# A weight block's residue made by POOL in two halves, each with its own semaphore, for a two-block network layer in split fp32

## What is computed

```python
def first_block(x, mem, ...):
    xn = rmsnorm(h, norm_mix_g); proj = xn @ w_in          # pool_mixer and sgu_mixer follow
    h = h + concatenate([y_pool, y_sgu]) @ w_out
    h = h + mem_cross_attention(rmsnorm(h, norm_xattn_g), mem, ...)   # wq, wk, wv, wo
    h = h + conv_ffn(rmsnorm(h, norm_ffn_g), w_up, conv_w, conv_b, w_down)
    return rmsnorm(h, final_norm_g)

def second_block(x, ...):
    h = rms_norm(x, norm1_g); proj = h @ w_in               # q, k, v, glu_a, glu_b
    x = x + concatenate([stick_breaking_attention(q, k, v), conv]) @ w_out
    gate, val = split(rms_norm(x, norm2_g) @ w_up)
    return x + (silu(depthwise_conv(gate)) * val) @ w_down
```

## Time and profile before

| | us |
|---|---|
| median of 3 runs | 1308.39 (1307.55 to 1308.89) |
| profiled execution, device time | 1306.23 |
| its span in the trace | 1304.5 |
| TensorE matmul busy (PE) | 1258.5 |
| VectorE busy (DVE) | 635.6 |
| POOL busy | 530.0 |
| ScalarE busy (ACT) | 485.4 |

### The profile page before, as it was taken

One profiled execution on the slowest core, in us unless ns is written; L12 is line 12 of the kernel. 1 busy time (PEld: TensorE's weight loads), 2 busy tenths in 40 slices (PEclk: granted clock), 3 DMA queues, 4 the chain that ended last, 5 costly groups with the idle time before them and its releaser, 6 DMA issues.

```text
span 1304.5 us, 16116 instructions
## 1 busy us (share of the span) xinstructions
PE 1258.5 (96%) x5574; PEld 1018.4 (78%) x5574; DVE 635.6 (49%) x882; ACT 485.4 (37%) x630; POOL 530.0 (41%) x244
## 2 busy tenths in 40 slices
PE   6899999999999999999979999799999999999999
PEld 6786888778888888888867776457888888888887
DVE  6829363353654155415585857694733313331332
ACT  6432342233443144314452234555533323332331
POOL 5854254223445344534454433000544353435343
PEclk9999999999999999999998999899999999999999
DMA  8432232112323222222232221000322232223222
GB/s 298 162 121 73 65 114 81 52 51 92 97 96 103 91 96 96 98 96 88 73 97 85 93 97 53 29 1 1 114 97 96 81 113 97 96 81 113 93 73 77
DMA packets 33313, 118.40 MB, mean 91 GB/s; under 512 B 3824, under 2 KB 3952, under 8 KB 32880
## 3 DMA queue, kind: packets, MB, share of 16 engines
q1 hardware_dynamic: 33120, 117.49, 27.1%
q10 hardware_dynamic: 144, 0.24, 0.1%
HBM read 115.61 MB, written 2.10 MB: 90 GB/s over the span
## 4 chain that ended last, share of the span: by engine, by line
PE 90%; DVE 6%; ACT 2%; issue 1%; DMA 0%; SPq 0%; DVEq 0%; ACTq 0%
PE ps L1028 25%; PE ps L1030 25%; PE ps L1029 25%; PE ps L1280 2%; DVE squares L625 2%; PE ps L1065 2%; PE ps L1066 2%; PE ps L1067 2%; PE ps L1263 1%; PE ps L1138 1%; PE ps L1160 1%; DVE slab L774 1%; DVE xg_lo L629 1%; PE ps L1307 1%; PE ps L1323 1%
## 5 line engine op out<-in xcount | busy, mean ns | idle before, releaser
L311 POOL TENSOR_TENSOR w_lo<-w_raw,w_hi 128x1024 fp32r<-128x1024 f32 x215 | 519.7, 2421 | 746.2 <-ACT w_hi L389 388.9
L1028 PE MATMUL ps<-xg_hi,w_hi 128*128 128x512 f32 x960 | 380.8, 397 | 10.4 <-DVE xg_lo L629 5.2
L1030 PE MATMUL ps<-xg_hi,w_lo 128*128 128x512 f32 x960 | 375.9, 392 | 0.0
L1029 PE MATMUL ps<-xg_lo,w_hi 128*128 128x512 f32 x960 | 375.7, 391 | 0.0
L1028 PE MATMUL ps<-y_hi,w_hi 128*128 128x512 f32 (+1 forms) x608 | 234.3, 385 | 13.6 <-DVE y_lo L629 10.8
L1030 PE MATMUL ps<-y_hi,w_lo 128*128 128x512 f32 (+1 forms) x608 | 231.5, 381 | 0.0
L1029 PE MATMUL ps<-y_lo,w_hi 128*128 128x512 f32 (+1 forms) x608 | 231.5, 381 | 0.0
L1028 PEld LDWEIGHTS ps<-xg_hi,w_hi 128*128 128x128 f32 x960 | 181.7, 189 | 51.4 <-DVE xg_lo L629 6.0
L1029 PEld LDWEIGHTS ps<-xg_lo,w_hi 128*128 128x128 f32 x960 | 181.8, 189 | 39.1 <-issue 1.7
L1030 PEld LDWEIGHTS ps<-xg_hi,w_lo 128*128 128x128 f32 x960 | 181.5, 189 | 38.3
L389 ACT ACTIVATE w_hi<-w_raw 128x1024 fp32r<-128x1024 f32 x136 | 143.1, 1052 | 160.3 <-PE ps L1030 126.5
(11 more groups left out here) (173 smaller groups left out, 1049.3 us busy)
## 6 DMA issues: line engine op xcount, KB each, us to landing
w_raw<-weights SPq DMA_DIRECT2D x200, 512.0 KB, 3.3
w_raw<-weights SPq DMA_DIRECT2D x16, 384.0 KB, 2.9
h<-x_t SPq DMA_DIRECT2D x2, 1024.0 KB, 11.7
out_t<-h SPq DMA_DIRECT2D x8, 256.0 KB, 2.0
slab<-mem_t SPq DMA_DIRECT2D x2, 512.0 KB, 6.1
slab<-mats_in SPq DMA_DIRECT2D x1, 1024.0 KB, 14.5
cols<-cols_in ACTq DMA_DIRECT2D x1, 231.0 KB, 4.3
corr<-corr_in SPq DMA_DIRECT2D x1, 32.0 KB, 14.4
```

What stands on the lines that cost most here:

```text
L311: nc.gpsimd.tensor_tensor(w_lo[:, s, :], w_raw[:, s, :], w_hi[:, s, :].bitcast(F32), ALU.subtract).then_inc(w_lo_ready, 1)
L1028: pe.matmul(out, w[0], x[0], start=first, stop=False)
L1029: pe.matmul(out, w[0], x[1], start=False, stop=False)
L1030: return pe.matmul(out, w[1], x[0], start=False, stop=last)
```

## The change

POOL subtracts in two instructions of 512 columns each; the first raises a new semaphore `w_lo_half`, the second the old `w_lo_ready`. VectorE's residue of block 0 is split in the same way. In `features` TensorE waits for `w_lo_half` at a block's start, and for `w_lo_ready` ahead of the first piece k of 4 or more; in `tokens` the first piece waits for `w_lo_half` and the second for `w_lo_ready`. SyncE's wait stays on `w_lo_ready`.

```diff
-        w_hi_ready, w_lo_ready = sem("w_hi_ready"), sem("w_lo_ready")
+        w_hi_ready, w_lo_half, w_lo_ready = sem("w_hi_ready"), sem("w_lo_half"), sem("w_lo_ready")
...
                 pool.wait_ge(w_hi_ready, b + 1)
-                nc.gpsimd.tensor_tensor(w_lo[:, s, :], w_raw[:, s, :], w_hi[:, s, :].bitcast(F32),
-                                        ALU.subtract).then_inc(w_lo_ready, 1)
+                for half, done in ((slice(0, BLK // 2), w_lo_half), (slice(BLK // 2, BLK), w_lo_ready)):
+                    nc.gpsimd.tensor_tensor(w_lo[:, s, half], w_raw[:, s, half], w_hi[:, s, half].bitcast(F32),
+                                            ALU.subtract).then_inc(done, 1)
...
-            nc.vector.tensor_tensor(w_lo[:, 0, :], w_raw[:, 0, :], w_hi[:, 0, :].bitcast(F32), ALU.subtract).then_inc(w_lo_ready, 1)
+            for part, done in ((slice(0, BLK // 2), w_lo_half), (slice(BLK // 2, BLK), w_lo_ready)):
+                nc.vector.tensor_tensor(w_lo[:, 0, part], w_raw[:, 0, part], w_hi[:, 0, part].bitcast(F32),
+                                        ALU.subtract).then_inc(done, 1)
...
                 if begin:
-                    pe.wait_ge(w_lo_ready, b + 1)
+                    pe.wait_ge(w_lo_half, b + 1)
...
                 for n, k in enumerate(order):
+                    if k >= DT // 2 and (n == 0 or order[n - 1] < DT // 2):
+                        pe.wait_ge(w_lo_ready, b + 1)
...
                 for s in range(4):
-                    pe.wait_ge(w_lo_ready, first + s + 1)
                     for kk in range(2):
+                        pe.wait_ge((w_lo_half, w_lo_ready)[kk], first + s + 1)
```

## The result

The changed kernel took 1300.08 us (1299.40 to 1300.61, 4 runs) beside 1307.97 us before (1306.75 to 1308.89, 4 runs): a ratio of 0.9942 [0.9927, 0.9957]. In two later comparisons the ratio was 0.9956 [0.9941, 0.9971] and 0.9958 [0.9944, 0.9971]. So it is faster, by 5.6 to 7.9 us, where I had forecast 2.6 us; 1300.08 lies under the low end of my range, 1302.6. The profiled execution took 1300.61 us (span 1298.9), 5.6 less than that of before.

The account below looks back on a forecast made before the run. TensorE, busy for 96% of the span, was taken as the bound, with VectorE setting the end in the hole. Terms -3.7 + 0.3 + 0.4 + 0.2, given as -2.6 us, put on the 1308.39 median: 1305.8 us, range 1302.6 to 1309.5.

Parts of the forecast that it names:

- the hole: Last down projection of the first feed-forward, 645 to 692 us: VectorE stands for half as long, -3.7 us.
- The stated effect: TensorE begins blocks with half the residue; its two `w_lo` waits of 2.6 us shrink, counted as no gain.
- the wait in mid-block: One more TensorE semaphore wait per block, 216 in all, taken as 0; third rival: stops the pipeline, 58 us, chance 0.03.
- 0.18 us a split: Extra POOL time for two instructions instead of one, making a half 1.29 us, between 1.20 and 1.40.
- the start: 25 to 45 us, where VectorE multiplies stand behind residues: plus 0.3 us, from -0.8 to 1.6.
- the pooling windows: 99 to 125 us, four residues among VectorE adds of two SBUF tiles: plus 0.4 us, from -0.3 to 1.1.
- The copy (L622): At the start, a VectorE copy newly stands behind part of the last half: 0.5 us taken, at most 1.29.
- the attention: Start of the attention, where L972 stands behind POOL and TensorE waits for its follower: plus 0.2 us, from 0 to 0.4.
- POOL keeps the port across both halves: First rival: VectorE cannot enter between halves, nothing gained, 18 pairs each 0.18 us longer, 1311.6 us; chance 0.12.
- the split costs 0.40: Second rival: the split costs near the power's 0.40 us, a half of 1.40, total 1309.2 us; chance 0.15.
- A clock gain in the hole: Fourth rival: shorter waits at 645 to 692 us keep TensorE at 2.4 GHz, up to 1.8 us more, 1304.0; chance 0.12.
- my first rival: POOL keeps SBUF's port through both halves, as consecutive POOL instructions are no barrier; 1311.6 us, chance 0.12.

Follow-up runs that it names:

- with the casts moved: Every residue in quarters as in the all-quarters kernel, with VectorE's two casts and mask multiply issued behind the first norm's reciprocal roots; 1301.86 us, ratio 0.9957 to before.

## Why the prediction was wrong

**What held.** The place, the mechanism and the order of size did. VectorE enters at the end of a half in the hole. The stated effect is worth nothing, as I had it (the split that waits for whole blocks gives 4.28 of 4.39 us), and so is the wait in mid-block (1.0005, unchanged). A half alone lasts 1.29 us in the median, the value I took; two take 2.54 where a whole one took 2.40, so 0.14 us for the instruction more. The estimate from the page GPSIMD Engine Reference of the Trainium skill, section 3.1 (Elementwise, side-by-side cycle accounting), was 0.30 and the measurement decides against it. That affine select is the nearer kin of the residue than the power, my reason for 0.18 over 0.40, no row shows; the 0.14 bears out the size alone.

**The step that failed: 0.18 us a split where the port changes hands.** I priced every half at 1.29 us, at the start and in the pooling windows too. But there POOL's next instruction has already started and stands at the port while VectorE works; my reading is that most of what a POOL instruction needs to begin lies under that wait. The timeline of VectorE at the start in after, one tile from L630 to L630, and TensorE's wait that answers to the last of the earlier trace rows:

```profile
33.78 1.45 DVE L630 SCALAR_TENSOR_TENSOR xg_lo<-h,cols,xg_hi 128x512 fp32r<-128x512 f32 x1
35.15 1.78 DVE L626 TENSOR_TENSOR squares<-squares 128x512 f32<-128x512 f32 x1
36.85 0.41 DVE L616 TENSOR_TENSOR slab<-ps,rstd_bc 128x256 f32<-128x256 f32 x1
37.19 1.45 DVE L630 SCALAR_TENSOR_TENSOR xg_lo<-h,cols,xg_hi 128x512 fp32r<-128x512 f32 x1
...
44.08 0.64 PE L1070 MATMUL ps<-w_hi,y_hi 128*128 128x512 f32 x1 [3.57 <-DVE slab L616]
```

A tile passes in 3.41 us: two VectorE instructions of 0.55 and two halves, so a half holds VectorE for (3.41 - 1.10) / 2 = 1.16 us and not 1.29. By the same reading the whole residue at 31.96 held it from 32.56 to 34.81, 2.25 us; the split costs 2 x 1.16 - 2.25 = 0.07 there, and not 0.18. A pair of tiles takes 6.82 us, where I had 7.36 against 7.45 before. The copy (L622) that newly stands did cost, 0.37 us by the matmul at 28.38, close to my 0.5. So the start came out at -0.7 where I had +0.3. At the pooling I had charged 0.4 by the same price and it gave back 0.2; that half was not measured by itself. At the attention I had charged 0.2, and no cost shows (-0.2). The start and the pooling came out near the lower bounds that I had put on them, -0.8 and -0.3, for a half of 1.20: in contention a half holds VectorE for less than that.

The kernel in quarters agrees, in the same place:

```profile
32.77 0.89 DVE L631 SCALAR_TENSOR_TENSOR xg_lo<-h,cols,xg_hi 128x512 fp32r<-128x512 f32 x1
33.59 1.23 DVE L627 TENSOR_TENSOR squares<-squares 128x512 f32<-128x512 f32 x1
34.74 0.41 DVE L617 TENSOR_TENSOR slab<-ps,rstd_bc 128x256 f32<-128x256 f32 x1
35.07 0.90 DVE L631 SCALAR_TENSOR_TENSOR xg_lo<-h,cols,xg_hi 128x512 fp32r<-128x512 f32 x1
```

A tile passes in 2.30 us there, so a quarter holds VectorE for (2.30 - 1.10) / 2 = 0.60 us, where four that nobody disturbs take 0.70 each. Whole, half or quarter, a POOL instruction holds a waiting VectorE for 0.10 to 0.15 us less than it takes alone.

**The hole, mis-sized by 0.7.** I let the next residue begin behind the first square sum, 3.79 us after the PSUM add. It begins 3.60 us after it, as in before (676.11 less 672.51; now 671.30 less 667.70), while the square sum still runs. So a pair of tiles gains 1.07 us and not 0.92. My bound of 4.7 for the hole held.

**Where I put the sum, and what the range left out.** My four terms as written add up to -2.8, and not to the -2.6 that I gave. As measured they add up to -5.5 (-4.4, -0.7, -0.2 and -0.2), near the -5.8 that I had worked out for a half of 1.20 and taken as the range's end; the start makes 1.0 of the difference, the pooling 0.6, the attention 0.4 and the hole 0.7. I put the sum on a median of three executions, 1308.39 us. Over all comparisons, 92 executions of before have a median of 1307.4 and the 17 of the changed kernel one of 1300.6; from 1307.4 the low end of my range would have been 1301.6. Single executions differ by several us, and the longer ones mostly have the lower mean granted clock: before took 1304.9 to 1306.8 us at 0.986 or 0.987 and 1308.6 to 1311.2 at 0.979 or 0.980, the changed kernel 1299.4 to 1301.9 at 0.986 or 0.987 and 1303.2 to 1303.5 at 0.980. But at 0.983, where half of those of before lie and none of the changed kernel's, before took anything from 1305.3 to 1309.0. At 0.986, the one clock with many of both, the medians lie 5.6 us apart, as the two profiled ones do. So about 5.6 us is what trace and equal clock show of the change; that the rest of the 7.9 us of the first comparison is its work too is not shown. My range took in the unknown prices and not this, so the first four executions after, at 0.986 and 0.987, could leave it by 2.5 us.

**The rivals.** That POOL keeps the port across both halves is not so for halves; that the split costs 0.40 isn't either, nor does the mid-block wait stop the pipeline. A clock gain in the hole didn't come: the sums of squares still take 3.57 us (3.58 before), and the granted clock of the hole is 0.89 against 0.91. The slow stretches elsewhere, which I had not thought of, moved single executions as much as that rival would have.

## What to carry to other kernels

Where VectorE stands behind GpSimd for SBUF's port, and VectorE sets the pace, cut the GpSimd instruction in the stretch where that happens: the loser waits for the one that is running, and there a split cost only 0.07 us here. Of unequal parts the short one first gave twice what the long one first did. Don't cut so fine that GpSimd loses its pauses, and look for what else is queued on VectorE while it has none: both shut-outs of VectorE for 17 us fell in such a run, though why is open. Price a resource that changes hands from rows in which it does, not from the duration of an instruction alone; and before a change of half a per cent is read from medians, lay the two traces beside each other matmul by matmul.

## What the runs showed of the hardware that was not expected

An unbroken run of short POOL instructions can shut VectorE out for as long as it lasts. The instruction at 56.67 us met 25 ends of a POOL instruction in that run and got in at none, in both kernels that had quarters and had it there; a copy at 75.93, with the casts moved, stood 3.04 us through four quarters. Yet in each of the same three profiles some 50 other VectorE instructions that came during an undisturbed quarter got in at its end, copies and 128-column ones among them, and with halves the casts of that very place did, at the end of one half (1.18 us in after), also where POOL had no pause. How early it came doesn't tell the cases apart: those shut out had started 0.43 and 0.67 us ahead of the first end, and of those that got in about half 0.2 us or more ahead, up to 0.7. Nor does the number of inputs. What does is open. The page GPSIMD Engine Reference of the Trainium skill, section 2.1 (Instruction dispatch), has it that a core starts the next instruction when its own share is done; the rows agree on the early start (each quarter starts 0.04 us before the last one ends), and neither the page nor they say when the port is given up, so that rule didn't make my first rival the case, as I had read it.

TensorE's slow stretches come and go. In each profile it ran at 1.2 GHz near the final squares, near 780 us and in the attention; near 16, 45, 127 and 816 us it did so in some kernels' profiles and not in others, each behind waits of TensorE, and such a stretch cost about 1.5 us (the 127 one in the pair of profiles above). The three profiles of the changed kernel have the same stretches; that they differ between executions of one kernel is told only by the mean granted clock, 0.980 to 0.987.
